# Three edits to a two-block transformer kernel: an earlier first gate of a scan, an earlier weight fetch, and an expert selection made in two parts

## The reference, cut to what matters

```
u = rmsnorm(h);  p = u @ w_in                      # parts dq dk dv | gq gk gv gg gr
z = gr @ gate_w + gate_b;  log_a = logsigmoid(z)/16 # gr has 16 columns, z has 256
og = gated linear attention in chunks of 64 (gq, gk, gv, log_a), times silu(gg)
da = differential attention, 4 heads x 8 blocks of 128 queries (dq, dk, dv)
h = h + concat(da, og) @ w_o
h = h + cross_attention(h, mem)                    # mem: 256 rows, rms-normed first
xf = rmsnorm(h)
group  = argmax(xf @ w_group + b_group)            # 4 groups
top 2 of the group's 8 experts by xf @ w_expert + b_expert
h = h + sum over the 2 chosen of gate * expert(xf)  # 32 experts, w_gate, w_up, w_down
```

## Time and profile before

| | us |
|---|---|
| median of 3 runs | 3118.78 (3115.3 to 3120.44) |
| the profiled execution | 3114.5 |
| its span | 3112.7 |
| PE busy in the span | 2920.2 (94%) |
| PEld busy | 2262.6 (73%) |
| DVE busy | 1855.2 (60%) |
| ACT busy | 1195.2 (38%) |
| POOL busy | 405.5 (13%) |

### The profile page before, as it was taken

One profiled execution on the slowest core, in us unless ns is written; L12 is line 12 of the kernel. 1 busy time (PEld: TensorE's weight loads), 2 busy tenths in 40 slices (PEclk: granted clock), 3 DMA queues, 4 the chain that ended last, 5 costly groups with the idle time before them and its releaser, 6 DMA issues. The chain is left out here.

```text
span 3112.7 us, 36756 instructions
## 1 busy us (share of the span) xinstructions
PE 2920.2 (94%) x15010; PEld 2262.6 (73%) x15010; DVE 1855.2 (60%) x2789; ACT 1195.2 (38%) x1850; POOL 405.5 (13%) x243
## 2 busy tenths in 40 slices
PE   8999898999999999999998998799898879999998
PEld 3444576887888888874556975794778868887777
DVE  5775656567444444572556437622224489999998
ACT  3110644232121211142333335422332357777776
POOL 1112300003000000021000000000000027433333
PEclk9999999999999999999999999999999989999999
DMA  9320100021111111122000010203002489999996
GB/s 326 102 81 21 45 1 1 28 68 55 54 41 55 43 52 41 54 73 91 1 1 28 28 41 1 82 29 134 1 1 64 183 302 368 389 387 384 380 379 255
DMA packets 129682, 363.39 MB, mean 117 GB/s; under 512 B 14475, under 2 KB 66985, under 8 KB 104929
## 3 DMA queue, kind: packets, MB, share of 16 engines
q1 hardware_dynamic: 112976, 330.19, 29.1%
q0 software_dynamic: 16528, 30.76, 2.7%
HBM read 356.69 MB, written 29.38 MB: 124 GB/s over the span
## 5 line engine op out<-in xcount | busy, mean ns | idle before, releaser
L180 PE MATMUL PS<-BIG 128*128 128x512 f32 (+10 forms) x2448 | 666.9, 441 | 44.3 <-ACT BIG L2279 17.1
L180 PEld LDWEIGHTS PS<-BIG 128*128 128x128 f32 (+4 forms) x2448 | 348.7, 189 | 295.9 <-issue 238.6
L2943 DVE TENSOR_TENSOR ML<-MR,MH 128x2048 fp32r<-128x2048 f32 x144 | 330.2, 2304 | 29.3 <-ACT MH L2938 28.9
L180 PE MATMUL PS<-MH,MX 128*128 128x512 f32 x1024 | 323.5, 398 | 11.6 <-DVE ML L2943 9.6
L2938 ACT CAST MH<-MR 128x2048 fp32r<-128x2048 f32 x144 | 275.4, 1914 | 93.8 <-DMA MR<-in_w_e_up 42.8
L180 PEld LDWEIGHTS PS<-MH,MX 128*128 128x128 f32 x1024 | 190.8, 190 | 56.3 <-DVE ML L2943 16.4
L180 PE MATMUL PS<-FWH,FHH 128*128 128x512 f32 x512 | 200.2, 391 | 5.1 <-DVE XR L1606 2.1
L180 PE MATMUL PS<-ML,MX 128*128 128x512 f32 x512 | 201.2, 393 | 0.0
L180 PE MATMUL PS<-FXH,FWH 128*128 128x512 f32 x512 | 200.1, 391 | 0.8 <-DVE FWL L1458 0.8
L180 PE MATMUL PS<-FXH,FWL 128*128 128x512 f32 x512 | 199.9, 390 | 0.0
L180 PE MATMUL PS<-FXL,FWH 128*128 128x512 f32 x512 | 199.8, 390 | 0.0
(11 more groups left out here) (477 smaller groups left out, 6065.9 us busy)
## 6 DMA issues: line engine op xcount, KB each, us to landing
MR<-in_w_e_gate SPq DMA_DIRECT2D x50, 1024.0 KB, 19.2
MR<-in_w_e_up SPq DMA_DIRECT2D x48, 1024.0 KB, 21.0
MR<-in_w_e_down SPq DMA_DIRECT2D x46, 1024.0 KB, 19.5
FWR<-in_w_ff SPq DMA_DIRECT2D x32, 1024.0 KB
XR<-in_w_e_down SPq DMA_DIRECT2D x18, 1024.0 KB, 18.7
BC<-in_w_ada SPq DMA_DIRECT2D x32, 512.0 KB, 3.7
XR<-in_w_e_up SPq DMA_DIRECT2D x16, 1024.0 KB, 21.1
XR<-in_w_e_gate SPq DMA_DIRECT2D x14, 1024.0 KB, 19.3
```

The lines of the kernel that those rows point to most:

```text
L180: ins = pe.matmul(o, l, r, start=(start and n == 0), stop=(n == len(pairs) - 1), skip_group_check=True)
L2943: dve.tensor_tensor(cut_at(ML, i), raw(i), cut_at(MH, i).bitcast(F32), ALU.subtract).then_inc(e.w_lo.up(), 1)
```

## The change

1. The gate. `gr` of the first half of the tokens is made right after the fourth GQK group, ahead of `pe_u_turn(1)`, into bank 4; that of the second half stays last, into bank 6. `pe_gate(0)` stands between the sixth and the seventh group, `act_gate(0)` behind ACT's sixth eviction, `dve_gate(0)` behind DVE's seventh. The memset of `GR` moves ahead of the groups. `pe_gate`, `act_gate` and `dve_gate` themselves are as before.
2. w_o. Two quarters are fetched by `sp_wo2_first`, which waits for the last d-projection group (`d_mm[48]`) as the items begin. The first quarter is cut at n = 32 of the items (`act_first_cut`, `dve_first_cut`), into `QWH` and a new half slot `QW0`. `project` gets a parameter `begun` for that. `act_mem` and `dve_mem` leave the items and stand behind row tile 0 and row tile 1 of `wo2`; `dve_da_normed(4..7)` stands behind DVE's eighth low part (`dve_middle`).
3. The router. `WRT` has 36 columns, POOL's memset goes, each tile's logits are made in two halves of 4 matmuls, the first of which waits for the first half of the transposes alone. Tiles 6 and 7 go to bank 4. The selection (`dve_choose`) runs for the tiles 0 to 5 after six logits, and then for 6 and 7.

```diff
@@ project @@
-                for i in range(4):
+                for i in range(0 if begun is None else 2, 4):
...
-                    if m == 7:
+                    if m == 7 and begun is None:
                         act_cut(0)
...
                     if m == 7:
-                        dve_cut(0)
+                        if begun is None:
+                            dve_cut(0)
+                        else:
+                            dve_middle()
@@ pe_gla_in @@
+        def pe_gate_rows(th):
+            P.wait_ge(*wgr_in[1])
+            P.wait_ge(*gq_v[1 + 6 * th])
+            mm(PS[0:16, 4 + 2 * th, :], [(WGR[:, k, :], XT[:, k, 512 * th:512 * th + 512])
+                                     for k in range(8)]).then_inc(g_gr.up(), 1)
...
                 if n == 4:
+                    pe_gate_rows(0)
                     pe_u_turn(1)
                     P.wait_ge(*u_done(15))
                     P.wait_ge(*u_done(16))
+                    P.wait_ge(*gr_ok[1])
+                if n == 6:
+                    pe_gate(0)
...
-            P.wait_ge(*wgr_in[1])
-            for th in range(2):
-                P.wait_ge(*gq_v[5 + th])
-                mm(PS[0:16, 4 + th, :], ...
+            pe_gate_rows(1)
@@ act_gla_in, dve_gla_in @@
+                if n == 5:
+                    act_gate(0)
...
+                if n == 6:
+                    dve_gate(0)
+            dve_gate_rows(1)
@@ items @@
+        def sp_wo2_first():
+            S.wait_ge(*d_mm[48])
+            for i in range(2):
+                sp.dma_start(QWR[:, 2048 * i:2048 * i + 2048]..., X["w_o_2"][0][:, 256 * i:256 * i + 256]...)
+        def act_first_cut():
+            A.wait_ge(*wo2_w[0][1])
+            act.copy(QWH[:, 0:2048], QWR[:, 0:2048]).then_inc(wo2_whi.up(), 1)
+        def dve_first_cut():
+            V.wait_ge(*wo2_whi[1])
+            dve.tensor_tensor(QW0, QWR[:, 0:2048], QWH[:, 0:2048].bitcast(F32), ALU.subtract).then_inc(wo2_wok.up(), 1)
...
-                if n == 24:
-                    act_mem()
+                if n == NI:
+                    act_first_cut()
...
-                if n == 27:
-                    dve_mem()
+                if n == NI:
+                    dve_first_cut()
             dve_da_inverse(16, 32)
-            for t in range(4, 8):
-                dve_da_normed(t)
@@ wo2 @@
+        def wo2_dve_middle():
+            for t in range(4, 8):
+                dve_da_normed(t)
+        def wo2_dve_after(t):
+            dve_rms(t, uc_sq, uc_ms, uc_std, uc_ok)
+            if t == 1:
+                dve_mem()
...
+            if t == 0:
+                act_mem()
@@ router @@
-        WRT = bc(1).rearrange("p (k n) -> p k n", k=8)
+        WRT = bc(1)[:, 0:288].rearrange("p (k n) -> p k n", k=8)
...
-            gps.memset(WRT, 0.0).then_inc(wr_zero.up(), 1)
...
+            if t >= 6:
+                P.wait_ge(*co2_ev[29])
+            P.wait_ge(*rt_ok[2 * t + 1])
+            mm(logits_at(t), [(RT[:, k, :], WRT[:, k, :]) for k in range(4)], stop=False)
             P.wait_ge(*rt_ok[2 * t + 2])
-            mm(PS[:, b, 128 * (t % 4):128 * (t % 4) + 128],
-               [(RT[:, k, :], WRT[:, k, :]) for k in range(8)]).then_inc(lg_mm.up(), 1)
+            mm(logits_at(t), [(RT[:, k, :], WRT[:, k, :]) for k in range(4, 8)], start=False).then_inc(lg_mm.up(), 1)
...
+        def dve_choose(a, b, known):
+            ...
+            V.wait_ge(*lg_mm[known])
+            for t in range(a, b, 2):
+                ...                        # bias added, two tiles at a time
+            dve_first_max(lg[:, :, 0:4], 4, ...); dve_one_hot(...)
+            ...                            # the chain as before, on tiles a to b
+                                 ALU.add).then_inc(mem_of.up(), 1)
...
-            V.wait_ge(*lg_mm[8])
-            ...                            # the chain over 8 tiles
+            dve_choose(0, 6, 6)
+            dve_choose(6, 8, 8)
```

More of the change, by code:

```diff
@@ L176, in C, with mm @@
             return CT[:, a:a + n]
-        def mm(o, pairs, start=True):
+        def mm(o, pairs, start=True, stop=True):
             for n, (l, r) in enumerate(pairs):
-                ins = pe.matmul(o, l, r, start=(start and n == 0), stop=(n == len(pairs) - 1), skip_group_check=True)
+                ins = pe.matmul(o, l, r, start=(start and n == 0), stop=(stop and n == len(pairs) - 1), skip_group_check=True)
             return ins
@@ L1216, in project @@
         def project(tag, x_mm, wd, src, scale_of, areas, first_load, pe_ready, act_ready, dve_ready, dve_evac, evac_done,
-                    dve_after, act_after, pe_after, order=range(8), third_first=False):
+                    dve_after, act_after, pe_after, order=range(8), third_first=False, begun=None):
             xh, xl, wr, wh, wl = areas
@@ L1231, in half, with low @@
                 return x[:, 2048 * (i % 2):2048 * (i % 2) + 2048]
+            def low(i):
+                return first_low if begun is not None and i == 0 else half(wl, i)
             def sp_project():
                 first_load()
-                for i in range(4):
+                for i in range(0 if begun is None else 2, 4):
                     if i >= 2:
@@ L1254, in pe_project @@
                     b = 4 + k_ % 4
-                    h_, l_ = (half(x, n).rearrange("p (k n) -> p k n", k=8) for x in (wh, wl))
+                    h_, l_ = (x.rearrange("p (k n) -> p k n", k=8) for x in (half(wh, n), low(n)))
                     P.wait_ge(*w_ok[n + 1])
@@ L2363, in program @@
         sp_da_back0()
+        sp_wo2_first()
         pe_da_att()
@@ L3240, in act_route @@
             act.activation(dd, dd, ACT.Exp).then_inc(dd_ok.up(), 1)
+        def dve_choose(a, b, known):
+            tl, n = slice(a, b), b - a
+            lg, em, e4, e32, first, second = (x[:, tl, :] for x in (LG, EM, eq4, eq, OH[:, 0:8, :], OH[:, 8:16, :]))
+            V.wait_ge(*lg_mm[known])
+            V.wait_ge(*br_in[2])
+            for t in range(a, b, 2):
+                pair = PS[:, 2 if t < 4 else 3 if t < 6 else 4, 128 * (t % 4):128 * (t % 4) + 256]
+                dve.tensor_tensor(LG[:, t:t + 2, :], pair.rearrange("p (t n) -> p t n", t=2)[:, :, 0:36],
+                                  BR.unsqueeze(1).to_broadcast([128, 2, 36]), ALU.add).then_inc(vs.up(), 1)
+            dve_first_max(lg[:, :, 0:4], 4, gm[:, tl], gi[:, tl], e4)
+            dve_one_hot(e4, gi[:, tl], 4, ALU.not_equal)
+            step().scalar_tensor_tensor(
+                out=em.rearrange("p t (g e) -> p t g e", g=4), in0=e4.unsqueeze(3).to_broadcast([128, n, 4, 8]),
+                scalar=MASK, in1=lg[:, :, 4:36].rearrange("p t (g e) -> p t g e", g=4), op0=ALU.mult,
+                op1=ALU.add).then_inc(vs.up(), 1)
+            dve_first_max(em, 32, m1[:, tl], i1[:, tl], e32)
+            dve_one_hot(first, i1[:, tl], 32, ALU.is_equal)
+            step().scalar_tensor_tensor(out=em, in0=first, scalar=NEG, in1=em, op0=ALU.mult, op1=ALU.add).then_inc(vs.up(), 1)
+            dve_first_max(em, 32, m2[:, tl], i2[:, tl], e32)
+            dve_one_hot(second, i2[:, tl], 32, ALU.is_equal)
+            step().tensor_tensor(MMB.rearrange("p (t n) -> p t n", t=8)[:, tl, :], first, second,
+                                 ALU.add).then_inc(mem_of.up(), 1)
         def dve_route():
```

128 lines of the change are left out of this document (57 added, 71 removed).

## The result

| | before | after |
|---|---|---|
| median, us | 3117.04 (4 runs, 3112.97 to 3120.44) | 3097.31 (4 runs, 3095.03 to 3097.84) |
| the profiled execution (its span) | 3114.5 (3112.7) | 3097.45 (3095.6) |

The ratio is 0.9933, with a 95% interval of 0.9919 to 0.9948: 19.7 us less. A second job gave 3095.25 against 3117.82 (0.9929, 0.9917 to 0.9942), 22.6 us less. The forecast was 3091, 27.5 less, in a range of 3083 to 3103.

What follows compares the result with a forecast made beforehand. PE, busy 2920.2 of 3112.7 us, was taken as the bound, the expert stage as bound by its weights. Terms 8.2 + 4.9 + 9.6 + 4.8 = 27.5 us, from 3118.8 to 3091; range 3083 to 3103.

Steps and rivals of the forecast that it cites:

- the first two rivals: Clock low at `wo2` and scan, 3095 to 3098, chance 0.16; early selection late or swallowed by experts' stream, 3096 to 3099, 0.10.
- part 1, to the first d-projection group: Scan's start: 24 records directly behind the gate rows, 2.83 us instead of 5.01, 4.93 us gap gone: 8.2 us.
- part 2a, the steps around n = 24 to 27: Items: moving mem work out saves 3.7 us of ACT's share and 1.2 of DVE's: 4.9 us, bounds 3 to 5.
- part 2b, start of the first group: First `wo2` group: earlier w_o fetch and cut let it start at 1989.8 instead of 1997.13: 7.3 us.
- part 2b, its clock: First `wo2` group takes 3.13 us instead of 5.37 if the clock stays up: 2.2 us.
- part 3, narrow logits: Router logits inside `co2`: each tile's 16 records gain 0.17 us, 0.8 in all, bounds 0 to 3.
- part 3, selection: Router: selection in two parts, done at 2487.6 instead of 2491.6: 4.0 us.
- the low bound: Start and clock of the first `wo2` group together: 6.1 us, with turns at the low clock and a slow first group.
- the clock stays low where I have it come back: Rival: low clock costs 3.5 us at `wo2`, up to 3.3 at the scan: 3095 to 3098; chance 0.16.
- for the case that part 3 gives nothing or costs 3: Router rival: selection not early or swallowed by experts' stream, gather beside prefetched pieces: 3096 to 3099; chance 0.10.
- The rival with the slower weight stream: Expert stage: changed offsets lower 382 GB/s, every 1% costs 6 us, 3124 at 362 GB/s; chance 0.06.

Runs made afterwards that it cites:

- before_again: The kernel before the change, unedited, profiled a second time: time 3123.45 us, span 3121.6.
- again: The changed kernel, unedited, run and profiled once more in a second job: 3095.25 us.
- gate_only: The kernel before with only the gate change (part 1): median 3112.40 us, ratio 0.9980.
- wo_only: The kernel before with only the w_o change (part 2): median 3106.35 us, ratio 0.9965.
- wide: The changed kernel with logits 128 columns wide again (36 used) and POOL's memset back: 3096.91 us (1 run).

## Why the prediction was right or wrong

Each part did in its own stage what was worked out for it, and the time lies in the range. The range is 20 us wide, though, and 3097.3 lies as well in the ranges of the first two rivals (3095 to 3098, 3096 to 3099); it is the stages that tell, not the time. The forecast's sum was 5 to 8 us too high. Taken against `before_again`, whose stages are those of the other runs, the stages give:

| step of the forecast | forecast | measured |
|---|---|---|
| part 1, to the first d-projection group | 8.2 | 7.9 |
| part 2a, the steps around n = 24 to 27 | 4.9 | 4.6 |
| the last item, behind its wait | 0 | -1.1 |
| part 2b, start of the first group | 7.3 | 7.6 |
| part 2b, its clock | 2.2 | 2.0 |
| part 3, narrow logits | 0.8 | 0.2 |
| part 3, selection | 4.0 | 4.3 |
| the first gather | 0 | -1.6 |
| the d-projection (-0.3) and the first `co2` group (-1.5) | 0 | -1.8 |
| sum | 27.5 | 22.1 |

22.1 agrees with the 19.7 and 22.6 of the medians. The two spans themselves differ by 26.0: another 1.2 us lie ahead of the in-projection and 2.6 in the expert stage, which goes from 593.5 to 598.1 over these profiles; neither is counted as the change's. Nor should the 1.5 of the first `co2` group be, which `again` does not have; without it the sum is 23.6. The last item is what remains of the whole items stage, 143.15 to 139.67 us, beside the 4.6. Point by point:

- Part 1 came as worked out: no gap, full clock, the cover on ACT held with 3.23 us left where I had counted 2. `gate_only` has the 24 records at 2.83 us too, but its whole gain is 6.0: its first `co2` group is slow as a whole, 108.2 us in that stage against 106.6, and one of its items takes 7.74 us where before has 6.09.
- Part 2a: the new place costs nothing. From first to last matmul `wo2` takes 93.87 us against 95.83, and the difference is the first group alone.
- Part 2b is the term that I took at its high end, and it came so. For the start of the group that is by the reason given: DVE's low parts run from 1971.56 for 5.66 us and the turns end with them. For its clock it is partly luck: I took 1.00 because `co2` has the same sequence of turns and kept 1.00, and in the ten other profiles without fills `co2` did not keep it. (The low bound was also added up wrong: 1997.13 less 1983.8, 6.05 and 0.9 leaves 6.4, not 6.1.) The rival "the clock stays low where I have it come back" did not happen at the scan or in the first `wo2` group, though the turns ahead of that group ran at 0.64 from 1974.0 to 1977.7 us.
- It happened elsewhere, and this is the step that failed. I took the clock behind waits that the change leaves alone from one profile, as if it went with them. The last item waits 3.21 us for DVE in both kernels, and behind it the 32 value records take 5.00 us now against 3.74 (the kernels with part 2 and no fills agree with after: the items stage is 139.7 to 139.8 us in `wo_only`, `again` and `wide`, and the records take 4.45 to 5.2). Why the same wait costs clock only behind part 2 is not shown. And in the stages behind, that profile was favourable by 5.4 us.
- Part 3, narrower logits: mis-sized. 16 records went from 2.05 to 1.98 us, 0.07 a tile and not 0.17, and `co2` got 0.2 us shorter, not 0.8. A single moving column at 0.10 us from start to start had been the right row to read, but in PE's queue the 128-column records already ran at 0.11.
- Part 3, the gather: I had put this among the rivals, for the case that part 3 gives nothing or costs 3. It cost 1.6 beside a full gain of the selection, so the rival's mechanism was there and belonged into the sum: the profile of before had DMA share 0.09 just ahead of the gather, and an earlier gather leaves that quiet stretch and meets the seventh and eighth piece.
- The rival with the slower weight stream is dead: 381 against 382 GB/s.

## What to carry to other kernels

Sum a change against a second profile of the kernel before, or at least compare each untouched stage between runs: here one profile made 5.4 us of untouched code look like a loss of the change. A shift that leaves the clock's falls at the same distance from the code says nothing about their moment: look where they lie before you conclude. Where PE waits 1 to 5 us for an operand in front of dense work, read the clock of the records behind the wait, not only the wait; products without use into the bank that is overwritten next bought 8.7 us here, provided that PE waits for the operand and not for the bank. When a small dependent transfer comes earlier, look at which large ones it then meets, and hold those whose data nobody needs yet.

## What the runs showed of the hardware

- The same code with the same waits ran at a granted clock of 0.97 in one execution and at 0.94 in the others over 272 to 278 us; with the waits filled, 0.99.
- Behind the same waits the clock fell 4.00 to 4.57 us (once 6.60) after the last `wo2` matmul began, and 0.53 to 0.71 us ahead of the first `co2` group or not at all; with that the group took 3.13, 4.40 or 5.49 us.
- An f32 matmul with 128 stationary columns goes on at about 0.11 us from start to start whether 128 or 36 columns move: 16 take 2.05 and 1.98 us.
- A gather of 128 rows of 4 KB took 7.3 to 9.1 us from issue to use beside 1 MB weight transfers, and 5.4 to 5.6 us in the three profiles without them. The weight stage behind it took 595.6 us where two of those transfers were issued some 13 us later and the next two some 5 us later, against 595.5.
